# The down projection of a feed-forward layer, from a plain product to seven products of halves

## The reference

```
h2 = _rmsnorm(x, g_pre_ffn)
ffn = (jax.nn.silu(h2 @ w_gate) * (h2 @ w_up)) @ w_down
x = x + _rmsnorm(ffn, g_post_ffn)
```

## Time and profile before

| | |
|---|---|
| time, median of 3 runs | 1290.61 us (1289.73 to 1292.06) |
| the profiled execution | 1288.78 us |
| its span, first to last instruction | 1286.9 us |
| mean granted TensorE clock | 0.986 |
| TensorE busy | 1244.6 us, 97% |
| VectorE busy | 838.0 us, 65% |
| ScalarE busy | 465.4 us, 36% |
| GpSimd busy | 37.2 us, 3% |

### The profile page before, as it was taken

One profiled execution on the slowest core, in us unless ns is written; L12 is line 12 of the kernel. 1 busy time (PEld: TensorE's weight loads), 2 busy tenths in 40 slices (PEclk: granted clock), 3 DMA queues, 4 the chain that ended last, 5 costly groups with the idle time before them and its releaser, 6 DMA issues.

```text
span 1286.9 us, 22506 instructions
## 1 busy us (share of the span) xinstructions
PE 1244.6 (97%) x9161; PEld 1221.6 (95%) x9161; DVE 838.0 (65%) x1476; ACT 465.4 (36%) x910; POOL 37.2 (3%) x52
## 2 busy tenths in 40 slices
PE   8799999999999999998999999999999999999996
PEld 8799999999988999998999999999999999999996
DVE  4766676675656685789777765666656443673584
ACT  5444443423120264454422232222322243433443
POOL 1000010101010000000000000000000000000001
PEclk9899999999997999999999999999999999999999
DMA  8321100103021333234333413233122485375383
GB/s 290 102 70 50 33 19 2 42 11 85 17 69 49 101 110 121 67 98 138 94 108 94 128 54 87 65 94 99 50 88 79 150 330 176 117 251 180 103 274 109
DMA packets 141877, 135.29 MB, mean 105 GB/s; under 512 B 15976, under 2 KB 124792, under 8 KB 141248
## 3 DMA queue, kind: packets, MB, share of 16 engines
q1 hardware_dynamic: 141776, 133.86, 33.2%
HBM read 111.26 MB, written 23.62 MB: 105 GB/s over the span
## 4 chain that ended last, share of the span: by engine, by line
PE 57%; DVE 8%; issue 1%; ACT 1%; DMA 0%; POOL 0%; POOLq 0%; DVEq 0%; ACTq 0%
PE pair L1495 32%; PE pair L1533 16%; PE pair L1454 5%; PE pair L1224 1%; DVE w_lo L2113 1%; DVE mix L1963 1%; PE pair L1353 1%; DVE mix L1988 1%; DVE w_lo L1921 1%; DVE qinv L1959 1%; DMA raw<-w_down_dram 0%; PE pair L1420 0%; DVE yo L2134 0%; POOL yo L840 0%; ACT w_hi L846 0%
## 5 line engine op out<-in xcount | busy, mean ns | idle before, releaser
L1495 PE MATMUL pair<-act_hi,w_hi 128*128 128x258 f32 x704 | 199.6, 284 | 4.3 <-DVE w_lo L1921 2.8
L1495 PE MATMUL pair<-act_hi,w_lo 128*128 128x258 f32 x704 | 198.9, 283 | 0.0
L1495 PE MATMUL pair<-act_lo,w_hi 128*128 128x258 f32 x704 | 198.8, 282 | 0.0
L1224 PE MATMUL pair<-act_hi,w_hi 128*128 128x344 f32 x528 | 180.4, 342 | 6.4 <-DVE act_lo L1586 3.5
L1533 PE MATMUL pair<-h_hi,w_hi 128*128 128x400 f32 (+1 forms) x528 | 170.4, 323 | 1.7 <-DVE h_lo L2116 1.7
L1224 PE MATMUL pair<-act_hi,w_lo 128*128 128x344 f32 x528 | 171.6, 325 | 0.0
L1224 PE MATMUL pair<-act_lo,w_hi 128*128 128x344 f32 x528 | 171.5, 325 | 0.0
L1533 PE MATMUL pair<-h_hi,w_lo 128*128 128x400 f32 (+1 forms) x528 | 170.0, 322 | 0.0
L1533 PE MATMUL pair<-h_lo,w_hi 128*128 128x400 f32 (+1 forms) x528 | 169.8, 322 | 0.0
L1495 PE MATMUL pair<-s_hi,w_lo 128*128 128x258 f32 x528 | 149.3, 283 | 0.0
L1495 PE MATMUL pair<-s_hi,w_hi 128*128 128x258 f32 x528 | 149.2, 283 | 0.0
(11 more groups left out here) (284 smaller groups left out, 2487.2 us busy)
## 6 DMA issues: line engine op xcount, KB each, us to landing
rawx<-w_down_dram SPq DMA_DIRECT2D x44, 512.0 KB, 3.9
raw<-w_up_dram SPq DMA_DIRECT2D x26, 512.0 KB, 4.8
rawx<-w_gate_dram SPq DMA_DIRECT2D x22, 512.0 KB, 5.0
raw<-w_down_dram SPq DMA_DIRECT2D x22, 512.0 KB, 3.9
raw<-w_in_dram SPq DMA_DIRECT2D x18, 512.0 KB, 4.1
hraw<-h_scratch SPq DMA_DIRECT2D x44, 200.0 KB, 4.0
h_scratch<-mix SPq DMA_DIRECT2D x23, 258.0 KB, 2.0
xc<-x_quads_dram SPq DMA_DIRECT2D x4, 1032.0 KB, 9.0
```

The costliest lines, as they stand in the source:

```text
L1224: mm = pe.matmul(out, a[:, k, :], b[:, k, cols(c)], start=(k == 0 and s == 0), stop=(k == KT - 1 and s == 2))
L1495: mm = pe.matmul(pair[psum_pair(n)][:, s, 0:QW], a[:, r, half + k, :], b, start=(k == 0 and i == 0), stop=(k == 3 and i == 2))
```

## The change

The down projection is made by seven products of halves (Strassen's scheme) too. Activations A are cut into row halves by inner halves, weights B into inner halves by output halves. Each product is 11 steps; in a step four output tiles by two row quarters by three forms, 24 matmuls of 258 columns, go into four pairs of PSUM banks. The order is M3, M1, M7, M5, M4, M2, M6; M6 is made twice over the 11 tiles, once for each quarter, so that its second quarter alone stands at the end.

| product | activations | weights | goes to |
|---|---|---|---|
| M3 | A11 | B12 - B22 | 12, 22 |
| M1 | A11 + A22 | B11 + B22 | 11, 22 |
| M7 | A12 - A22 | B21 + B22 | 11 |
| M5 | A12 + A11 | B22 | 12, and 11 subtracted |
| M4 | A22 | B21 - B11 | 11, 21 |
| M2 | A21 + A22 | B11 | 21, and 22 subtracted |
| M6 | A21 - A11 | B12 + B11 | 22 |

GpSimd makes the weight sums (`sum_b`), among them in M4 those for M6, which stay split (`t_hi`, `t_lo`), and the activation sums of M5, M2 and M6; VectorE makes the activation sums of M1 and M7 (`sum_a` in its `down_lo`). A11, A22, B11 and B22 stay in the chip's memory after their first load. When a product ends, its four pairs of banks are copied or added into the output quarters, by ScalarE (`y_copy`) and VectorE (`y_add`); the next product's matmuls wait for each pair (`pair_taken`). The old row x2 is added by GpSimd (`add_x2`) for three of the row quarters, and for the last one by GpSimd (first five tiles) and VectorE (three).

```diff
-DCH = ((0, 400), (400, 400), (800, 232))
+HELD = 4
+POOL_TAIL = 5
+DOWN = ("M3", "M1", "M7", "M5", "M4", "M2", "M6")
+STEPS = [(p, m) for p in DOWN[:-1] for m in range(HALVES)] + [("M6", m) for _ in range(2) for m in range(HALVES)]
+FULL = (len(DOWN) - 1) * HALVES
+AT = {p: HALVES * i for i, p in enumerate(DOWN)}
+TURN_AT = {AT["M4"] + 3 + m if m < 8 else FULL + m - 8: m for m in range(HALVES)}
...
+    HALF_SLOT = [max(v for v in range(FULL) if v % DH == n) for n in range(DH)]
+    def a_free(v):
+        if v < DH:
+            return prod_used("P6" if v < 2 else "P7")
+        if v < FULL:
+            return step_used(v - DH)
+        h = v - FULL
+        return step_used(v - 2 * DH) if h >= 2 * DH else step_used(HALF_SLOT[h // 2])
+    def b_free(v):
+        return step_used(v - DH) if v >= DH else prod_used(("P2", "P5", "P3", "P4")[v])
...
@@ the SP queue @@
+        for v in range(DR, NSTEP):
...
+            load_a(v)
+            if v < FULL:
+                load_w(v)
+            k = v - (AT["M2"] + DR + 1)
+            if 0 <= k < KT:
+                sp.wait_ge(sem("a_sum"), a_sums(AT["M2"] + k + (k >= 4)))
+                sp.dma_start(x2a(k, 1)[:, 0], x2_d[:, k, HALF:ROWS]).then_inc(sem("x2_in"), 16)
...
@@ GpSimd @@
+        def sum_b(v):
+            p, m = STEPS[v]
+            if not b_summed(v):
+                return
+            pool.wait_ge(sem(B_SEM[v % DR]), b_count[v])
+            x = b_in[v % DR]
...
+            if p == "M4":
+                pool.tensor_tensor(t_in32[:, m], t_in32[:, m], b11(m), ADD)
+            y = b11(m) if B_OF[p][1] == "11" else b22(m)
+            pool.tensor_tensor(x, x, y, B_OF[p][2]).then_inc(sem("b_sum"), 1)
...
+        for v in range(NSTEP):
...
+            if v < FULL:
+                sum_b(v)
+            sum_a(v)
+            n = v - (FULL - 3)
+            if 0 <= n < 8:
+                if n == 0:
+                    pool.wait_ge(sem("x2_in"), 16 * KT)
+                add_x2(n // 4, 2 * (n % 4))
...
@@ ScalarE @@
+        def down_hi(v):
+            p, m = STEPS[v]
+            if v < FULL:
+                if b_summed(v):
+                    act.wait_ge(sem("b_sum"), b_sums(v))
+                act.wait_ge(*b_free(v))
+                copy(b_ring[v % DH][0], b_source(v)).then_inc(sem("d_hi_done"), 1)
...
+            act.wait_ge(*a_free(v))
+            copy(a_tile(v, 0), a_source(v)).then_inc(sem("h_hi_done"), 1)
...
+            if v == FULL + 2:
+                y_copy("M2")
...
@@ TensorE @@
+        def tile_step(v, mt):
+            p, m = STEPS[v]
+            if m == 0:
+                pair_taken(v, mt)
+            for s in range(2) if v < FULL else (sub(v),):
+                mm = down(v, mt, s)
...
@@ VectorE @@
+        def down_lo(v):
+            p, m = STEPS[v]
+            if p in ("M1", "M7"):
+                sum_a(v)
+            if v < FULL:
+                dve.wait_ge(sem("d_hi_done"), v + 1)
+                hi, lo = b_ring[v % DH]
+                dve.tensor_tensor(lo, b_source(v), hi.bitcast(F32), SUB).then_inc(sem("d_split"), 1)
+            dve.wait_ge(sem("h_hi_done"), v + 1)
+            if v in TURN_AT:
+                t = TURN_AT[v]
+                dve.tensor_tensor(t_lo[:, t], t_in32[:, t], t_hi(t).bitcast(F32), SUB)
+            dve.tensor_tensor(a_tile(v, 1), a_source(v), a_tile(v, 0).bitcast(F32), SUB).then_inc(sem("h_split"), 1)
...
+            if v == AT["M4"] + 2:
+                for mt in range(4):
+                    y_add("M5", "11", SUB, (mt,))
+                    y_add("M5", "12", ADD, (mt,))
...
+            if v == FULL + 2:
+                y_add("M2", "22", SUB)
...
+        y_add_last(1)
+        y_turn(3)
+        scale_y(3, range(KT))
```

More of the change, by code:

```diff
@@ L769, in _ @@
             elif q + 2 == FT:
[L770 to L773, removed]
+                for v in range(DR):
+                    load_a(v)
+                    load_w(v)
             if q % 2:
@@ new lines, in y_copy, with y_squares @@
+        def y_copy(p):
+            dst = {"M3": "12", "M1": "11", "M4": "21"}.get(p)
+            for mt in range(4):
+                act.wait_ge(sem("acc_mm"), 4 * DOWN.index(p) + mt + 1)
+                out = y_tile(dst, mt) if dst else y_tmp[:, mt]
+                copy(two(out), dpair(mt)[:, :, 0:QW]).then_inc(sem("y_cp"), 1)
+        def y_squares(c, r):
+            n = SQUARES.index((c, r))
+            if n >= 2:
+                act.wait_ge(sem("y_sum"), n - 1)
+            for mt in range(4):
+                made = {"12": ("M5", "12", mt), "11": ("M4", "11", mt), "21": ("M2", "21", mt), "22": ("M6", "22", mt, r)}[c]
+                act.wait_ge(sem("y_ev"), ADD_AT[made])
+                act.activation(ysq[:, 4 * r + mt], y_tile(c, mt, r), ACT.Square).then_inc(sem("y_sq"), 1)
@@ new lines, in y_stat @@
+        def y_stat(b, out):
+            pe.wait_ge(sem("y_sum"), (3, 4, 7)[b])
+            pe.matmul(out[:, 0:QW], ones[:], ysum[:, b % 2], start=True, stop=True).then_inc(sem("y_stat"), 1)
+        for v in range(NSTEP):
+            p, m = STEPS[v]
+            if v < FULL:
+                pe.wait_ge(sem("d_split"), v + 1)
+            pe.wait_ge(sem("h_split"), v + 1)
+            held = p == "M2" and m < HELD
+            for mt in range(3 if held else 4):
+                tile_step(v, mt)
+            if held and m == HELD - 2:
+                pair_taken(AT["M2"], 3)
+                y_stat(0, dpair(3)[:, 0])
+                y_stat(1, dpair(3)[:, 1])
+            if held and m == HELD - 1:
+                pe.wait_ge(sem("y_std"), 2)
+                for late in range(HELD):
+                    tile_step(AT["M2"] + late, 3)
+            if v == FULL + HALVES + 3:
+                pe.wait_ge(sem("y_ev"), ADD_AT["M6", "22", 0, 0])
+                y_stat(2, dpair(0)[:, 0])
@@ L1562, in _ @@
+        pe.wait_ge(sem("y_sum"), 6)
+        out = dpair(1)[:, 0, 0:QW]
+        pe.matmul(out, ones[:], ysum[:, 1], start=True, stop=False)
+        for mt in range(4):
+            pe.wait_ge(sem("y_sq"), 4 * len(SQUARES) - 3 + mt)
+            mm = pe.matmul(out, ones[:], ysq[:, 4 + mt], start=False, stop=(mt == 3))
         mm.then_inc(sem("y_stat"), 1)
@@ new lines, in y_turn, with scale_y @@
+        def y_turn(b):
+            dve.wait_ge(sem("y_std"), b + 1)
+            if b >= 2:
+                dve.wait_ge(sem("y_t"), KT * (b - 1))
+            then(dve.reciprocal(yinv[:, b % 2], ystd[:, b % 2]))
+        def scale_y(b, ks):
+            for k in ks:
+                x = yo[:, k, block_rows(b)]
+                dve.scalar_tensor_tensor(out=x, in0=x, scalar=gain[:, POST_FFN, k:k + 1], in1=yinv[:, b % 2],
+                                         op0=ALU.mult, op1=ALU.mult).then_inc(sem("y_t"), 1)
@@ L2144, in _ @@
             down_steps(n)
[L2145 to L2146 removed]
+        for v in range(2, NSTEP):
             down_lo(v)
[L2148 to L2165 removed]
```

548 lines of the change are left out of this document (374 added, 174 removed).

## The result

The changed kernel takes 1309.32 us (median of 4 runs, 1308.6 to 1312.97) against 1290.61: a ratio of 1.015, 95% interval 1.0129 to 1.017. It is 18.7 us slower. The forecast was 1280.1 us, range 1261 to 1297: the sign is wrong, and the time is 12 us above the range.

A forecast was written before the change was run, and what follows sets the result against it. TensorE was taken as the bound: 222.0 us of matmuls plus column sums, waits and slow spells made 248.1 against 258.8; 10.7 gained, 0.2 lost in the tail, so 1290.6 - 10.5 = 1280.1 us, range 1261 to 1297.

The forecast's parts named there:

- the 36.8 us: Down projection's matmuls on TensorE: 1848 of 258 columns take 222.0 us against 258.8 before, so 36.8 us to be had.
- The exclusion: VectorE's two-SBUF-input instructions and GpSimd's SBUF reads lock each other out, so their times add; 1.07 us per GpSimd sum.
- lateness shows at the takeover: At product ends, taking out accumulators stands behind the next product's step 2 split; only 0.2 us of slack.
- The x2 chain at M2: M2's step 9 sum queues on GpSimd behind x2's loads and addition: 7.1 us from split 8 to 9, 3.5 late.
- gaps in M3: Sign against the forecast: TensorE gaps in M3, from loads, would show it wrong; M3 was given no lateness.
- hidden with 0.6 to spare: M3's loads: a round of about 8 us over three steps of 2.88, landing in 3.9 us, costs nothing.
- likeliest case: Whole kernel: exclusion costs as priced, 10.5 us gained, 1280.1 us; range 1271 to 1288, chance 45%.
- first rival: Whole kernel: exclusion costs little as GpSimd's sums fall into VectorE's waits; 29.1 us gained, 1261.5 us, chance 22%.
- slow spell: Matmuls after idle stretches of some us run at the lower clock, 1.6 us each; two taken, 3.3 us.
- The case without exclusion: Stage 232.3 us, with 1.8 at M4, 3 for x2's loads, 2.6 at M6; whole 1261.5 us, chance 22%.
- Rival 2: M1, M7, M4, M2: GpSimd is the bound with 55 sums, at 1.67 us each; slower, 1303 us, chance 21%.
- Rival 3: Late splits at M4 and M2 (4.5 and 5 us) cost double; no change to be told, 1290 us, chance 12%.

The follow-up runs named there:

- sp_early: Changed kernel with the loads of M3's steps 3 and 4 issued ahead of the last two stores: 1304.5 us, ratio 1.0118.
- no_lock: Changed kernel with GpSimd writing constants for about as long in place of its sums, reading nothing from SBUF (sums left out): 1281.67 us, ratio 0.9942.
- take1: Changed kernel with accumulators taken out behind step 1 of the next product instead of step 2: 1300.56 us, ratio 1.0074.
- all_fix_no_lock: Changed kernel with earlier taking-out, earlier M3 loads, x2 additions two steps later, and constants written in place of GpSimd's sums: 1265.57 us, ratio 0.9835.
- take1_vec: Changed kernel with all sums on VectorE, taking-out one step earlier and M3's loads of steps 3 and 4 earlier: 1291.09 us, ratio 1.0014.
- the three edits: Changed kernel with taking-out one step earlier, M3's loads ahead of the last stores, and x2 additions two steps later: together 1292.63 us, ratio 1.0029.
- x2_late: Changed kernel with GpSimd's first eight additions of the old row x2 six steps later: 1304.24 us, ratio 1.0104.

## Why the prediction was wrong

Forecast and measurement of the stage, by its parts:

| | forecast | measured |
|---|---|---|
| bare matmuls, 1848 | 222.0 | 222.0 |
| column sums | 1.3 | about 1.3 |
| M3 | 0 | 13.2 |
| M1 and M7 | 3 | 5.2 |
| M5 | 1.8 | 2.4 |
| M4 and M2 | 4.5 + 8.5 | 9.4 + 21.9 |
| M6 | 3.7 | 6.9 |
| of these at the lower clock | (3.3, apart) | 14.0, within |
| stage | 248.1 | 280.9 |
| tail | 14.0 | 14.85 |

The measured excess of a product is its length less 31.7 and holds its part of the lower clock and of the column sums; the forecast's 3.3 and 1.3 stood by themselves. It holds the gap at the start of the next product as well, which the forecast mostly put to that next product: 6.5 of M3's 13.2, 4.7 of M4's 9.4 and 4.1 of M2's 21.9 are such gaps.

**What held.** 1848 matmuls of 0.120 us: the 36.8 us were there. The exclusion, with GpSimd's sum at 1.26 (1.29 measured). That lateness shows at the takeover: an edit of one step there gave 8.8 us. The x2 chain at M2: 7.4 us from split 8 (1232.8) to split 9 (1240.2), for 7.1. And the forecast named gaps in M3 as a sign that it is wrong.

**The step that failed first: "hidden with 0.6 to spare. The first splits are made before 1014.25 as now."** It priced M3's loads by their mean landing of 3.9 us and looked for no queue in front of them. The loads of step 3 stand behind the feed-forward stage's last store, go out in a burst and land in 5.2 us, so the round is longer than three steps. The earlier trace rows could give the landing but not the queue; the order in SP's program could. M3 took 13.2 us over its bare time for the forecast's nothing. Not all of that is the queue: sp_early takes 4.1 off, the exclusion accounts for 6.1 (no_lock), the earlier taking-out for 3.9 (take1), each measured by itself; together they leave nothing (31.7 in all_fix_no_lock).

**The exclusion was priced too low, 15.8 for 27.6.** The forecast's distance between its likeliest case and its first rival is 18.6 us: 15.8 in the stage (248.1 less 232.3, one slow spell in it) and 2.8 in the tail, which no_lock leaves alone. So the price is 15.8 for 27.6. The 15.8 had nothing in M3 (6.1 measured), where the work fitted in the step but not in the round of a load, a sum, a copy and a split, which lengthens by each wait. M4 had 4.5 (8.1 measured). Joint work alone is too small a measure for it here: what a wait lengthens is the chain of a round, also where each engine has time left. The tail as a whole was forecast nearly right, 14.0 for 14.85.

**The case without exclusion was also mis-sized, by 17.4 us: 1261.5 + 2.8 for the tail is 1264.3 forecast, 1281.7 measured.** (11.8 and 17.4 are the 29.2 us by which the forecast missed.) M2 keeps 13.2 us there and M3 7.2, where the forecast had 3 (and 2.6 for M6's start) and 0. In no_lock's M2 the chain from split 8 to split 9 takes 9.1 us for the forecast's 7.1, with TensorE's longest gap, 6.2:

```profile
1212.79 1.10 DVE L2442 TENSOR_TENSOR a_ring<-a_in,a_ring 128x516 fp32r<-128x516 f32 x1 [5.80 <-ACT a_ring L1086]
1213.81 2.71 DVE L2507 SCALAR_TENSOR_TENSOR mix<-mix,gain,act_lo 128x258 f32<-128x258 f32 x4
```

M6's start adds 3.6 and the lower clock 2.5. In the changed kernel a further piece comes on top, for which the forecast had nothing: behind split 9 four scalings stretch from 1.67 to 5.25 us and delay split 10 to 1248.2, 8.0 us after split 9, and TensorE then runs at the lower clock (0.85 over the product).

**The spells at the lower clock: 3.3 for 14.0.** The forecast's two spells were 24 matmuls each, 48, at 0.067 us more for each; there were 149, at 0.094. They follow the gaps, which were 43.4 us where the forecast's terms (3, 1.8, 4.5, 8.5, 3.7) make 21.5. take1_vec, with one gap of 1.1 us in four products, has a single such matmul there. One more term is short: five steps of 2.0 us against 1.44 are 2.8 us at M6, and the forecast takes 1.1 without saying what covers the rest.

**The rivals.** Rival 2 gave the right side and a near number, 1303, by the wrong mechanism: GpSimd's sum was 1.29 us, not 1.67. Rival 3, late splits at M4 and at the start of M2 that cost double, is not borne out either: the gaps within M4 (3.1) and at M2's start (4.7) were 7.8 us, where the forecast had 4.5 + 5. What was dear stands behind them, the gaps at steps 7 to 10 of M2 (10.1), at M6's start (4.1) and the lower clock in M2 (6.8), and in M3. No rival had these together.

**Left open.** With every sum's exclusion out and the three edits in, M2 keeps 4 us and M6 10 over their bare time. The additions of x2 are seen in both, but no kernel left them out, so their whole price is not shown. No kernel had both M2 and M6 at their bare time. Nor did any run tell apart which of the three edits gives what in the whole, beyond take1, sp_early and x2_late by themselves.

## What to carry to other kernels

When a stage's step shrinks (here from 24 matmuls of 400 columns to 24 of 258, 2.88 us), work out the round of its ring as a chain, load, sum, copy, split, divided by the depth of the ring, not only each engine's share of a step; here 9.8 for 8.64 us cost the whole lead within one product. Read the program of the queue around the seam of two stages: what stands ahead of the first load that isn't in the ring yet. Where accumulators are taken out in order behind the next product's splits, every delay shows there; try the taking-out one step earlier before moving work between engines.

## What the hardware did that was not expected

A series of short VectorE scalings with two operands in SBUF (258 columns, 0.42 us each) beside an unbroken series of GpSimd additions runs at GpSimd's pace, 1.3 us each: four took 5.25 us instead of 1.67. Here the exclusion cost the short instructions a factor of 3.1, where the mean split went from 0.700 to 1.046 us, a factor of 1.5.

GpSimd writing constants, with no read, for as long as its sums had taken left VectorE's splits at 0.700 us. Exclusion comes with its reads: the Trainium skill's page SBUF — State Buffer, "Who interferes with whom", says that a VectorE instruction with two SBUF inputs doesn't contend with a GpSimd instruction that only writes, and the run agrees.

Two loads of 256 KB that stand next to each other in the queue landed differently. From the transfers between 1015 and 1045 (KB each, median us to landing):

```profile
rawx<-w_down_dram SPq DMA_DIRECT2D x8, 256.0 KB, 3.3
act_hi<-w_down_dram SPq DMA_DIRECT2D x8, 256.0 KB, 5.1
```

The second is issued 0.48 us behind the first and takes 1.8 us longer, and it is the one that GpSimd's sums mostly wait for (26.6 us in all behind `act_hi`, 17.9 behind `rawx`). Why it lands later is open; no run varied it.
